# Loading some weight pieces of an expert kernel in halves of 1 MB, one after another

## The reference

```python
def expert_block(args):
    xb, e = args
    u = xb @ w_in[e] + b_in[e]            # 1024 -> 2048
    return _clamped_swiglu(u) @ w_out[e] + b_out[e]   # 1024 -> 1024
...
out = jnp.zeros((n_tok, d), h.dtype).at[tok_pad].add(ys * g_pad[:, None])
```

## Time and profile before

| | us |
|---|---|
| median of 3 runs | 1867.73 (1866.98 to 1868.55) |
| profiled execution, time | 1869.45 |
| profiled execution, span | 1868.0 |

### The profile page before, as it was taken

One profiled execution on the slowest core, in us unless ns is written; L12 is line 12 of the kernel. 1 busy time (PEld: TensorE's weight loads), 2 busy tenths in 40 slices (PEclk: granted clock), 3 DMA queues, 4 the chain that ended last, 5 costly groups with the idle time before them and its releaser, 6 DMA issues.

```text
span 1868.0 us, 51572 instructions
## 1 busy us (share of the span) xinstructions
PE 1820.3 (97%) x22829; PEld 1661.3 (89%) x22829; DVE 1107.4 (59%) x2818; ACT 463.6 (25%) x1358; POOL 218.6 (12%) x250
## 2 busy tenths in 40 slices
PE   7999999998999999999999999999999999999997
PEld 4665865567999999999999999999999999999996
DVE  2754776775655555656565655556574756555465
ACT  2204654431212121212121212121221212122213
POOL 2003000000101010101010101101020101011012
PEclk9999999999999999999999999999999999999998
DMA  8981111126979797969797997979897999999996
GB/s 322 356 182 47 49 75 51 46 79 255 348 269 358 269 366 286 363 252 368 258 364 287 366 341 275 387 270 380 285 389 267 377 341 359 340 353 336 349 340 216
DMA packets 150229, 523.98 MB, mean 281 GB/s; under 512 B 10042, under 2 KB 15826, under 8 KB 150002
## 3 DMA queue, kind: packets, MB, share of 16 engines
q1 hardware_dynamic: 131202, 467.68, 68.4%
q0 software_dynamic: 17200, 52.59, 8.4%
q10 hardware_dynamic: 1600, 0.36, 0.1%
HBM read 485.34 MB, written 34.21 MB: 278 GB/s over the span
## 4 chain that ended last, share of the span: by engine, by line
PE 94%; DMA 2%; DVE 2%; issue 1%; ACT 1%; POOL 0%; SPq 0%; POOLq 0%; DVEq 0%; ACTq 0%
PE ps L1820 49%; PE ps L1842 24%; PE ps L1682 6%; PE ps L1603 4%; PE ps L1690 3%; PE ps L1581 1%; PE ps L1536 1%; PE ps L1553 1%; PE ps L1632 1%; PE ps L1624 1%; PE ps L1599 1%; PE ps L1662 1%; PE ps L1503 1%; DMA xr<-acc_d 1%; PE ps L1716 0%
## 5 line engine op out<-in xcount | busy, mean ns | idle before, releaser
L1820 PE MATMUL ps<-xr,ring 128*64 128x128 f32 (+6 forms) x4864 | 502.3, 289 | 0.7 <-issue 0.7
L1820 PEld LDWEIGHTS ps<-xr,ring 128*128 128x128 f32 (+1 forms) x4864 | 498.5, 168 | 2.6 <-issue 1.3
L1842 PE MATMUL ps<-U,ring 128*64 128x120 f32 (+11 forms) x6656 | 470.0, 270 | 2.8 <-ACT U L911 2.4
L1842 PEld LDWEIGHTS ps<-U,ring 128*64 128x64 f32 (+1 forms) x6656 | 464.2, 149 | 4.7 <-issue 4.1
L1820 PE MATMUL ps<-U,ring 128*64 128x120 f32 (+4 forms) x8448 | 432.0, 259 | 10.0 <-issue 9.8
L1820 PEld LDWEIGHTS ps<-U,ring 128*64 128x64 f32 (+1 forms) x8448 | 425.9, 139 | 15.1 <-issue 14.2
L1387 DVE TENSOR_SCALAR U<-ps,U 128x120 f32<-128x120 f32 (+11 forms) x256 | 90.9, 355 | 468.1 <-PE ps L1820 466.0
L1324 DVE STREAM_TRANSPOSE xr<-U 32x256 f32<-32x256 f32 (+1 forms) x484 | 227.9, 471 | 91.6 <-DMA U<-xn_d,U 84.7
L897 ACT ACTIVATE U<-U 128x120 f32<-128x120 f32 (+11 forms) x256 | 80.1, 313 | 811.6 <-DVE U L1387 800.4
L1336 DVE STREAM_TRANSPOSE xr<-U 32x256 f32<-32x256 f32 (+1 forms) x484 | 230.0, 475 | 9.3
L911 ACT ACTIVATE U<-ps,U,modT 128x120 f32<-128x120 f32 (+11 forms) x256 | 112.4, 461 | 263.8 <-PE ps L1842 253.6
(11 more groups left out here) (248 smaller groups left out, 1194.7 us busy)
## 6 DMA issues: line engine op xcount, KB each, us to landing
ring<-in_moe_w SPq DMA_DIRECT2D x191, 2048.0 KB, 13.3
U<-in_w_mod SPq DMA_DIRECT2D x8, 2048.0 KB, 11.9
ring<-in_w_mod SPq DMA_DIRECT2D x3, 2048.0 KB, 18.9
acc_d<-xr SPq DMA_DIRECT2D x10, 512.0 KB, 3.5
xr<-in_x SPq DMA_DIRECT2D x8, 512.0 KB, 9.4
ring<-in_w_qkv SPq DMA_DIRECT2D x2, 2048.0 KB, 11.0
ring<-in_w_o SPq DMA_DIRECT2D x2, 2048.0 KB, 8.3
xn_d<-U SPq DMA_DIRECT2D x8, 512.0 KB, 2.6
```

The lines of the kernel that those rows point to most:

```text
L1820: last = pe.matmul(bank(j % 4)[lo:hi, s * 256:s * 256 + n], w[:, k, s, (j % 2) * P + lo:(j % 2) * P + hi], columns_of(r)[:, k, 0:n], start ...
L1842: last = pe.matmul(bank(4 + m % 4)[lo:hi, 0:n], w[:, k, (m % 4) * P + lo:(m % 4) * P + hi], actT[:, k, 0:n], start=(k == 0), stop=(k == KT ...
```

## The change

The pieces that are asked for while a narrow slot runs (asked_in_narrow: in slots up to 23, the last piece of a narrow slot, and those pieces of a wide slot whose step lies below 16) are loaded in two halves of 1 MB. Before the first half SyncE waits until the piece before it, in its order, has landed; before the second half it waits until the first has landed. That is piece 5 of the twelve narrow slots 1 to 23, pieces 0 and 1 of the wide slots 2 to 12, and pieces 0 to 3 of the wide slots 14 to 22, 44 pieces. All others are loaded as before, at the same steps. The counts that TensorE waits for follow the number of transfers.

```diff
+        def asked_in_narrow(r, p):
+
+            if r == 0 or r > LAST_MIXED + 1:
+                return False
+            return p == NPIECE - 1 if not wide(r) else load_step(r, p) < 16
+
+        def load_step(r, p):
+
+            if wide(r):
+                return (steps_light if WIDTHS[r - 1] <= LIGHT else steps_spread)[p]
+            return (steps_full if r > 2 and WIDTHS[r - 2] <= LIGHT and wide(r - 1) else steps_to)[p]
+
+        def transfers_of(r, p):
+
+            return 2 if (r, p) == (0, 0) else 2 if asked_in_narrow(r, p) else 1
+
         def loads_of(r, p):
-            return (r + 2) * 16 if p == 0 else (r + 1) * 16
+            return 16 * sum(transfers_of(q, p) for q in range(r + 1))
...
-                        sp.wait_ge(s_mm, (r - 1) * 16 + steps[p])
+                        sp.wait_ge(s_mm, (r - 1) * 16 + load_step(r, p))
...
+                    elif asked_in_narrow(r, p):
+                        before_it = (r, p - 1) if p else (r - 1, NPIECE - 1)
+                        sp.wait_ge(s_wl[before_it[1]], loads_of(*before_it))
+                        load_runs(sp, e, p, 0, NRUN // 2, s_wl[p])
+                        sp.wait_ge(s_wl[p], loads_of(r - 1, p) + 16)
+                        load_runs(sp, e, p, NRUN // 2, NRUN, s_wl[p])
                     else:
                         load_piece(sp, e, p, s_wl[p])
```

More of the change, by code:

```diff
@@ L64 @@
 LIGHT = 104
+LAST_MIXED = max(r for r in range(E) if WIDTHS[r] > P)
 def before(r, narrow_count, wide_count):
```

## The result

The changed kernel takes 1916.33 us (median of 5 runs, 1914.43 to 1918.1), the kernel before beside it 1867.83 us: a ratio of 1.0257, interval 1.0243 to 1.0271, 48.5 us slower. The profiled execution has a span of 1916.5 us.

A forecast was written before the change was run, and what follows sets the result against it. TensorE was taken to bound the kernel, with DMA time free only in narrow slots. The profiled 1869.45 us plus 64 for dead time and 8 for packets gave 1941.5, median 1940; forecast 1905 to 1960, full range 1875 to 1991.

The forecast's parts named there:

- What bounds the kernel: TensorE, busy 97% of the span; its pauses in narrow slots, taken for late instructions, were worth 13.4 us at most.
- the free DMA time of the narrow slots: DMA time not busy in narrow slots: 72.9 us in slots 1 to 11, 49.2 us in 13 to 21; wide slots full.
- The price of a half: Each 1 MB half in the split pieces takes 5.0 to 5.6 us, 2.25 to 2.85 us of it dead.
- Rival 1: Narrow slots: the pauses go and the halves fit, 1854 us, if a half takes under 4.5 us; chance 0.10.
- The term for instruction packets inside halves: Halves in narrow slots land later when an instruction packet shares an engine: 8 us taken, 0 to 66 possible.
- my own sum: Dead time of 86 halves, less gathers in the gaps, free DMA time and the lead: 64 us, plus 8 for packets.
- The 1.5 us of gathers in the gaps: Of 3.3 us of row gathers and scatters in a narrow slot, 1.5 us was let fall into the gaps.
- the lead of 17 us: Pieces asked for in narrow slots arrive early for the wide slot, so 17 to 18 us of delay cost nothing, once.
- Pauses that vanish give nothing back: Where transfers set the pace, curing narrow-slot pauses saves nothing, so the 13.4 us weren't taken off the loss.
- The steady state: Once the lead is used up in the first two spread slots, TensorE waits about 14 us per pair of slots.
- the marks I named: Profile signs: 70 to 90 us of weight waits, wide slots 14 to 22 longer by 8 to 15 us, narrow-slot pauses mostly gone.
- Rival 3: Worse than forecast, above 1960 us: instruction packets lengthen halves; a lower TensorE clock after waits priced at nothing; chance 0.20.

The follow-up runs named there:

- the two repairs: Kernel before, asked pieces waiting for the one before up to slot 12, then only pieces 5 and 0: whole pieces 1859.68 us; with halves up to slot 6, 1857.12 us.
- the spread group alone: The change only in narrow slots 13 to 23 and wide slots 14 to 22, against the kernel before: 1906.4 us, ratio 1.0223.
- the light group alone: The change only in narrow slots 1 to 11 and wide slots 2 to 12, against the kernel before: 1861.46 us, ratio 0.9988.

## Why the prediction was right, point by point

**What bounds the kernel: right.** The pauses were real, were placed where the chain had them, and were worth about what the slot lengths said: 13.4 us by the table, 9.0 and 11.6 us in the two repairs. That they are the instruction stream, which the prediction only took to be so, the traces bear out. That the free DMA time of the narrow slots decides, not the share of TensorE, was right too: the spread group alone, which had 49.2 us free for 50 halves (and slot 23's two), costs 43 us, and the light group alone, which had 72.9 us for 36, costs nothing.

**The price of a half: right, with a high middle.** I had 5.0 to 5.6 us for a half and 2.25 to 2.85 us of it dead; measured were 5.34 and 2.6 on the average, 4.93 and 2.18 in halves with nothing beside them. Rival 1 needed 4.5 us; the fastest of the 44 first halves took 4.8. One of the two halves that the price rested on was misread: the second one of slot 0 wasn't alone on its queue, a transfer of 2 MB followed 0.6 us after it.

**The term for instruction packets inside halves, 8 us (0 to 66): too small.** One packet lengthens a half by 0.25 us and two by 1.3 us, as said above; over 88 halves that makes some 21 us, an estimate from the 44 that could be timed. With the gap of 2.18 us and this term, my own sum is 86 x 2.18 + 21 - 16.5 - 122.1 - 17 = 53 us, for 48.5 measured. The gathers that lengthen some halves stand in the 16.5. So of the 24 us by which 1940 was too high, some 19 come from these two terms together, and 4 to 5 us are left.

**How much of that is luck.** That so little is left is in part luck. Two errors work against each other in it, the next one and the one on the clock: a gain that I left out and a loss that I priced at nothing. The 1.5 us of gathers in the gaps was an assumption, and no run measures it. Nor is the lead of 17 us measured by itself, and it wasn't used over two slots, as I wrote. By my own numbers ten halves leave 10 x 2.55 - 1.5 - 7.0 = 17 us over in the first spread slot, all of the lead; and in the kernel with the spread group alone the first wide slot, 14, is 3.9 us longer already.

**"Pauses that vanish give nothing back": wrong for half of the way.** As long as the lead lasts, TensorE sets the pace, and the cure counts: 7.4 us from the start of slot 1 to that of slot 9. I had let the lead go into the sum as 17 us once, but not the cure that came with it. It was hidden in the total because the light group paid it back in slots 9, 10 and 13.

**The steady state: right in kind.** "From then on TensorE waits about 14 us in each pair of slots": slots 14 to 22 with their narrow neighbours are 7 to 12 us longer per pair. Of the marks I named, four showed: nearly all waits on weights stand in front of the wide slots 14 to 22 and inside them, with one of 4.7 us in front of slot 10; the slots from 24 on are unchanged; the pauses of the narrow slots are gone; and there are 88 transfers of 1 MB, of which the 44 that could be timed took 4.8 to 7.6 us, 5.34 on the average. Three showed in part or not at all. The waits sum to 50 us, not 70 to 90, in line with the smaller loss. The wide slots 14 to 22 are 6.1, 7.2, 6.8, 9.1 and 12.1 us longer, three of them under the 8 to 15 I had. And narrow slots of the spread group have a DMA share of 0.69 to 0.77, not 0.5 to 0.65, while the wide ones fell to 0.85. I had thought of the gaps as staying in the narrow slot; SyncE does its work in order, so the chain of ten halves starts late and reaches into the wide slot.

**Rival 3, the lower clock: priced at nothing, and it costs 4 to 8 us.** The granted clock is 0.94 to 0.98 in the slots 9, 10, 20 and 22: TensorE was at the 1.2 GHz level for a part of each. Slot 10 shows the price alone. TensorE is busy for all of its 57.33 us, so nothing is waited for inside it, and it takes 2.4 us more than the 54.92 us before; ahead of it stands a wait of 4.71 us. In the slots 20 and 22 four of the eight stretches of products between two waits are longer than the 8.11 us of the others, by 1.4 to 1.6 us each:

```profile
1373.31 9.75 PE L1839 MATMUL ps<-xr,ring 128*128 128x144 f32 x64 [3.84 <-issue]
1383.55 8.11 PE L1839 MATMUL ps<-xr,ring 128*128 128x144 f32 x64 [0.49 <-DMA ring<-in_moe_w]
1394.40 9.49 PE L1839 MATMUL ps<-xr,ring 128*128 128x144 f32 x64 [2.74 <-DMA ring<-in_moe_w]
...
1506.74 9.63 PE L1839 MATMUL ps<-xr,ring 128*128 128x144 f32 x64 [4.73 <-DMA ring<-in_moe_w]
```

That makes 8.4 us of slower products. My reason for the zero, that TensorE waits for weights anyway, holds for those of them with a wait behind them, as between the first two lines. It doesn't for slot 10 and for the last product of slot 22, 3.9 us together. The slots 14, 16 and 18, at 1.00 throughout, are 6 to 7 us longer without it, so the clock isn't the main cause.

## What to carry to other kernels

Price a wait between transfers by the gap it leaves, the time from one issue to the next less the moving time, and hold the sum against the free time of the DMA engines in that stretch: two gaps in a piece cost 48.5 us here where one cost nothing. If small pauses come from something that queues behind large transfers, look at how many stand in a row before making them smaller. A fixed order on one queue carries every delay into the next stretch, so a stretch with no free time pays for the one before it.

## What the runs showed of the hardware

TensorE can run out of instructions while large transfers move on another queue: each pause ends 1.2 to 1.7 us after an instruction packet of 16 KB has landed. How long the pauses are goes more with whether two transfers follow each other than with their size: 10.0 us before, 7.7 with halves in a row, 1.8 with lone whole pieces, 0.2 with lone halves, none with half as many instructions. The Trainium skill ("DMA: Bandwidth & Descriptors", Queues, rings and completion order) has each DMA engine take turns between its queues, one packet of typically 9 to 17 descriptors at a time. By that I would have expected a second transfer behind the first to make no difference to an instruction packet; the 10.0 and 1.8 us don't agree with it. When a packet was asked for is in no trace, so how long one waits isn't shown.

Products of float32 with 128 columns of weights take 42.84 us for a slot of 88 columns of data and 42.87 for one of 120, so something other than the data's width, 112 ns for each of 384 products, sets their pace; in two blocks of 64 the same slots take 29.3 and 39.4 us.
